# Two transformer blocks on one core: the order of ScalarE's and VectorE's work between the heads of the third block

## The chip, the cores and the metric

The kernel runs on one core of a Trainium2 chip. The metric is the device time of the whole kernel in microseconds, as the median of several runs; lower is better. TensorE, VectorE, ScalarE, GpSimd and SyncE each run their own program in order and meet at semaphores.

## The reference, cut to what matters

The input is one sequence of 256 tokens of width 1024, with a memory of 256 tokens of the same width. A first part (two layers with HGRN2 mixing and chunk-band attention, each followed by a SwiGLU) comes before the stretch that the change touches. The part that it touches is this (fp32 throughout):

```
proj = rms_norm(x) @ w_in            # q (8 heads of 64), k and v (2 heads), u, g
u, g = gelu(proj[u]), gelu(proj[g])
attn = sliding_window_attention(rms_norm(q), rms_norm(k), v, sinks)
sg   = u * spatial_gating(rms_norm(g))
x    = x + concat(rms_norm(attn), rms_norm(sg)) @ w_out
q    = rms_norm(rms_norm(x) @ w_cq)  # 4 heads of 256
k, v = rms_norm(mem_n @ w_ck), mem_n @ w_cv    # mem_n = rms_norm(mem)
x    = x + softmax(q k^T / 16) v @ w_co
x    = x + moe(rms_norm(x))          # 32 experts, 2 per token
```

## The kernel before

Every linear layer is computed from pieces of 128 output columns. A piece of weights comes from HBM into a ring of six slots (two pieces each). ScalarE rounds it to a high half (`hi_upto`, line 807), VectorE subtracts to get the low half (`lo_upto`, line 1268), and TensorE makes three products for each of eight chunks (48 matmuls for two pieces, lines 1999, 2023 and 2045). There are four buffers of split pieces, so the split of piece w can start when TensorE is done with piece w-4. Two result banks `lin` take turns; a pair of pieces must be drained by ScalarE or VectorE before the next pair but one can begin.

The activation operand `u` is also in two halves: ScalarE writes the high one and counts `u_hi`, VectorE the low one and counts `u_lo`.

The third block is called W, the cross attention X. TensorE's program goes through the heads of W two at a time: `scores_two`, a transpose of the probabilities (`turn_`, line 2309), `outputs_two` (line 2356). Between heads it does the 16 pieces `FILL` (keys `ck`, then values `cv`, of the memory), the spatial gates (lines 2522 and 2527) and sums of squares: FILL 0 and 1 after the first scores, 2 and 3 after turn 0, the gates after turn 1, 4 and 5 after turn 2, 6 and 7 after turn 3, 8 and 9 after turn 4, 10 and 11 after turn 5, 12 and 13 after turn 6, 14 and 15 after the last outputs. In the text "FILL n" is the nth of these pieces, and "pair n" is FILL 2n and 2n+1. The change leaves TensorE's program as it is.

For a head of W, VectorE scales and masks the scores and takes maxima (`scores`, lines 1584 to 1600), ScalarE does the exponentials (`exps`, line 973), VectorE divides (`probs`, lines 1609 and 1612), TensorE turns, ScalarE copies the turned block (`copy`, line 984) and later takes an output pair (`drain`, line 1154's group). Between heads both engines call `between_w(i)`, which ends with splits of the next FILL pieces and, on ScalarE, with `memory(i)`, which drains finished pairs: a square and a copy for the keys (lines 1070 and 1071), a copy for the values (line 1074). How far they may go at i is given by

```
def filled(i):
    return 2 * (i + 2) if i < 1 else min(2 * (i + 1), 14) if i < HW else 16
```

Before W, `in2_act` drains the seven pairs of the input projection; the last is a gelu (line 1116). Then ScalarE writes the memory operand (line 1122) and VectorE its low half (line 1742). After W come the output projection `out2` (`add_gated`, line 1351), the norm `cross`, the queries `cq` and X, whose keys need six steps `key_norm(0)` to `key_norm(5)` on VectorE: four reciprocals (line 1701) and two products (line 1705). TensorE's first X scores (line 2299) wait for both products.

Of the kernel before, what the change touches and what calls it, by code (L numbers as in the profile page):

```python
# [29 lines left out]
DC = D // P  # L30
# [174 lines left out]
def two_blocks(nc, x, c, mod_w, mod_b, norm_mix, norm_ffn, ffn_w_in, ffn_w_out, a_w_in, a_w_out, a_lb,  # L205
# [15 lines left out]
    with ExitStack() as ctx:  # L221
# [575 lines left out]
        def _(act):  # L797
# [164 lines left out]
            def attention_act(kind, hi_out, between=lambda i: None):  # L962
# [30 lines left out]
                if kind == "X":  # L993
                    for i in range(n + 2):
                        if i < n:
                            exps(i)
                        if 1 <= i <= n:
                            copy(i - 1)
                        if i >= 2:
                            drain(i - 2)  # L1000
                        between(i)
                    return
                for j in range(n // 2 + 1):
# [59 lines left out]
            def memory(i):  # L1063

                hi_upto(min(FILL[0]["w"] + filled(min(i - 1, HW)) + 3, LAST["cv"] + 2))
                while 2 * drained[0] + 2 <= min(filled(min(i - 1, HW)), 14):
# [23 lines left out]
            def in2_act():  # L1090
                for n, pair in enumerate(pairs("in2")):
                    if n == 6:
                        act.wait_ge(w_dup, 1)
                        act.activation(kdup, acc[:, 0:2, :], ACT.Copy).then_inc(w_dc, 1)
                    result(pair)
# [21 lines left out]

            in2_act()
            wait_out(act, jobs["in2"][-1])
            act.wait_ge(x_tc, 2)  # L1120
            for c_ in range(DC):
                act.activation(u[:, 0, c_, :], memT[:, c_, :], ACT.Copy, scale=vec("norm_mem_2", c_)).then_inc(u_hi, 1)

            def between_w(i):

                if i == 0:
                    for b in range(TB):
# [132 lines left out]
        def _(dve):  # L1260
# [79 lines left out]
            def add_gated(job, gate):  # L1340

                for n, pair in enumerate(pairs(job)):
# [13 lines left out]
                    ins.then_inc(lin_out["dve"], 1)  # L1356
                    if job == "a_out" and n < 2:
# [216 lines left out]
            def attention_dve(kind, lo_out, between=lambda i: None):  # L1574
# [46 lines left out]
                if kind == "X":  # L1621
                    scores(0)
                    for i in range(n + 2):
                        if i == 1:
                            probs(i)
                        if i + 1 < n:
                            scores(i + 1)
                        if i < n and i != 1:
                            probs(i)
                        if i >= 2:  # L1630
                            drain(i - 2)
                        between(i)
# [105 lines left out]
            lo_upto(LAST["in2"] + LOOKAHEAD)  # L1738
# [6 lines left out]
            wait_out(dve, jobs["in2"][-1])  # L1745
# [3 lines left out]
            def between_w(i):  # L1749

                if i == 0:
                    dve.wait_ge(w_std, 3)
# [33 lines left out]
            attention_dve("W", None, between_w)  # L1786
# [8 lines left out]
            for n, p in enumerate(jobs["cq"][:6]):  # L1795
                lo_upto(p["w"] + LOOKAHEAD)
                key_norm(n)
# [7 lines left out]
                lambda i: lo_upto(jobs["co"][(1, 3)[i]]["w"]) if i < 2 else None)  # L1805
# [998 lines left out]
```

## Time and profile before

| | |
|---|---|
| median of 3 runs | 1487.49 us (1486.2 to 1488.25) |
| the profiled execution | 1483.92 us, span 1481.9 us |
| TensorE matmul busy | 1437.8 us, 97% of the span |
| VectorE busy | 755.2 us, 51% |
| ScalarE busy | 565.2 us, 38% |
| mean granted TensorE clock | 0.986 |
| moved from and to HBM | 404.14 MB, mean 273 GB/s |

TensorE is busy nearly all the time. The third block begins near 820 us of the span, the output projection near 900, the cross attention near 950 and the experts near 1030. In the timeline a row gives the start, the busy time, the engine, the line, and in brackets the idle time just before it and what ended it. The granted clock is a share of 2.4 GHz: 1.00 is 2.4 and 0.50 is 1.2.

### The profile page before, as it was taken

The numbers are of one execution on the slowest core, as the hardware profiler recorded it, in microseconds if no ns is written. First come the engines' busy times: TensorE is split into PE (matmuls) and PEld (weight loads), VectorE is DVE, ScalarE is ACT, GpSimd is POOL, SyncE is SP. The second block draws the span as 40 slices with busy tenths as digits, with TensorE's granted clock in tenths as the row PEclk, the third lists the DMA queues.
The fourth block names the chain that finished last, engine by engine and source line by source line (L and its number), as shares of the span: only waits on it lengthen the run. The fifth ranks groups of instructions, "written<-read, shape, count | busy, mean of one in ns | idle before, by whom it ended". The sixth has DMA issues, their size and how long they took to land. (4 is left out here: it accounts for less than half of the span.)

```text
span 1481.9 us, 26323 instructions
## 1 busy us (share of the span) xinstructions
PE 1437.8 (97%) x11240; PEld 1211.5 (82%) x11240; DVE 755.2 (51%) x1194; ACT 565.2 (38%) x885; POOL 28.6 (2%) x47
## 2 busy tenths in 40 slices
PE   7999999999999999999999899999999999999997
PEld 4998899999999879999999789888666566566664
DVE  3968767876776656555555655644122122122121
ACT  2522235343454555444444664451212212212211
POOL 0100000000001010000000000010000000000000
PEclk9999999999999999999999999999999999999999
DMA  9996455979769514665645336426999999999996
GB/s 370 309 322 211 155 174 196 328 279 319 280 225 327 177 52 164 207 222 204 210 132 168 118 114 236 163 62 253 413 424 427 425 427 425 428 427 425 426 425 263
DMA packets 155378, 404.14 MB, mean 273 GB/s; under 512 B 5107, under 2 KB 123152, under 8 KB 133906
## 3 DMA queue, kind: packets, MB, share of 16 engines
q1 hardware_dynamic: 152960, 396.90, 71.1%
q0 software_dynamic: 1648, 5.18, 1.2%
q8 instruction: 76, 1.25, 0.4%
q10 hardware_dynamic: 674, 0.64, 0.1%
q14 instruction: 20, 0.16, 0.0%
HBM read 401.63 MB, written 1.07 MB: 272 GB/s over the span
## 5 line engine op out<-in xcount | busy, mean ns | idle before, releaser
L1999 PE MATMUL ps<-u,wsplit 128*128 128x256 f32 x3744 | 461.7, 284 | 5.3 <-DVE wsplit L1268 5.3
L1999 PEld LDWEIGHTS ps<-u,wsplit 128*128 128x128 f32 x3744 | 452.8, 192 | 11.9 <-DVE wsplit L1268 6.4
L1268 DVE TENSOR_TENSOR wsplit<-arena,wsplit 128x1024 fp32r<-128x1024 f32 x258 | 312.5, 1226 | 198.7 <-ACT wsplit L807 198.5
L807 ACT ACTIVATE wsplit<-arena 128x1024 fp32r<-128x1024 f32 x258 | 270.1, 1056 | 294.9 <-PE ps L1999 150.8
L2666 PE MATMUL ps<-arena 128*64 128x256 f32 x1408 | 155.9, 379 | 1.1 <-DVE arena L1897 0.8
L2666 PEld LDWEIGHTS ps<-arena 128*64 128x64 f32 x1408 | 101.6, 137 | 60.8 <-issue 12.6
L1902 DVE TENSOR_TENSOR arena<-arena,ps 128x256 f32<-128x256 f32 x32 | 13.5, 422 | 235.9 <-ACT arena L1216 223.8
L2261 PE MATMUL ps<-hid,wsplit 128*128 128x256 f32 x1056 | 130.7, 283 | 0.3 <-DVE hid L1524 0.3
L2261 PEld LDWEIGHTS ps<-hid,wsplit 128*128 128x128 f32 x1056 | 128.3, 192 | 0.5 <-DVE hid L1524 0.5
L1221 ACT ACTIVATE arena<-ps 64x512 f32<-64x512 f32 x62 | 36.6, 591 | 141.4 <-PE ps L2688 140.7
L2045 PE MATMUL ps<-wsplit,u 128*128 128x256 f32 x672 | 83.2, 284 | 1.8 <-ACT arena L1074 1.6
L2045 PEld LDWEIGHTS ps<-wsplit,u 128*128 128x128 f32 x672 | 81.3, 192 | 2.9 <-DVE wsplit L1268 2.2
L2688 PE MATMUL ps<-arena 128*64 128x512 f32 x336 | 76.7, 598 | 0.5 <-ACT arena L1218 0.5
L2666 PE MATMUL ps<-late,arena 128*64 128x256 f32 x640 | 71.0, 379 | 1.0 <-DMA late<-in_w 1.0
L1336 DVE SCALAR_TENSOR_TENSOR arena<-arena,cact 128x2048 f32<-128x2048 f32 (+1 forms) x33 | 70.1, 2125 | 0.2
L2666 PEld LDWEIGHTS ps<-late,arena 128*64 128x64 f32 x640 | 45.8, 137 | 28.8 <-issue 5.6
L1216 ACT ACTIVATE arena<-ps 128x256 f32<-128x256 f32 x31 | 11.9, 384 | 148.2 <-PE ps L2666 148.2
L2023 PE MATMUL ps<-u,wsplit 128*128 128x256 f32 x480 | 61.0, 287 | 5.0 <-DVE u L1742 2.1
L2023 PEld LDWEIGHTS ps<-u,wsplit 128*128 128x128 f32 x480 | 59.0, 191 | 7.5 <-DVE wsplit L1268 3.9
L2651 PEld LDWEIGHTS ps<-arena 128*128 128x128 f32 x512 | 59.5, 192 | 5.8 <-issue 5.8
L2651 PE MATMUL ps<-arena 128*128 128x128 f32 x512 | 63.8, 278 | 0.0
L1912 DVE SCALAR_TENSOR_TENSOR y_split<-arena,y_split 128x1024 fp32r<-128x1024 f32 x15 | 19.3, 1285 | 80.7 <-ACT y_split L1228 80.7
(369 smaller groups left out, 1376.3 us busy)
## 6 DMA issues: line engine op xcount, KB each, us to landing
arena<-in_w SPq DMA_DIRECT2D x64, 2048.0 KB, 22.4
late<-in_w SPq DMA_DIRECT2D x30, 2048.0 KB, 23.5
arena<-in_mod_w SPq DMA_DIRECT2D x48, 1024.0 KB, 7.0
arena<-in_ffn_w_in SPq DMA_DIRECT2D x44, 1024.0 KB, 5.9
arena<-in_ffn_w_out SPq DMA_DIRECT2D x22, 1024.0 KB, 5.0
arena<-in_a_w_in SPq DMA_DIRECT2D x16, 1024.0 KB, 8.6
arena<-in_kv_mod_w SPq DMA_DIRECT2D x8, 1024.0 KB, 4.9
arena<-in_kv_w SPq DMA_DIRECT2D x8, 1024.0 KB, 7.2
```

The source lines that it names most:

```text
L807: act.activation(piece_buf(p, 0), piece_src(p), ACT.Copy).then_inc(hi_done, 1)
L1221: act.activation(y_sb[64 * k:64 * k + 64, 512 * j:512 * (j + 1)], ps[64 * j:64 * j + 64, 6, :], ACT.Copy).then_inc(m_yc, 1)
L1268: dve.tensor_tensor(piece_buf(p, 1), piece_src(p), piece_buf(p, 0).bitcast(F32), ALU.subtract).then_inc(lo_done, 1)
L1336: ins = dve.scalar_tensor_tensor(out=total, in0=rows, scalar=cact[:, k, 7:8], in1=total, op0=ALU.mult, op1=ALU.add)
L1912: dve.scalar_tensor_tensor(out=y_split[:, 1, :], in0=y_sb, scalar=slot_gate, in1=y_split[:, 0, :].bitcast(F32), op0=ALU.mult, op1=ALU.subt ...
L1999: mm = pe.matmul(o, w_[:, k, :], u[:, x_, k, :], start=first, stop=last)
L2023: mm = pe.matmul(lin[p["out"] % 2][:, p["half"], :], piece_buf(p, lo)[:, k, :], u[:, x_, k, :], start=(at == 0 and n == 0 and p["half"] == 0),
L2045: mm = pe.matmul(lin[p["out"] % 2][:, b, :].rearrange("p (c n) -> p c n", c=2), u[:, x_, k, P * b:P * (b + 1)], wsplit[:, first_buf:first_ ...
L2261: mm = pe.matmul(acc[:, c_, :], piece_buf(p, lo)[:, k, P * jj:P * (jj + 1)], hid[:, fi % 2, x_, k, :], start=(i == 1 and c_ % 2 == 0 and k ...
L2651: mm = pe.matmul(ps[:, 6 + half, P * c_:P * (c_ + 1)], hn_tok[:, b, P * (4 * half + c_):P * (4 * half + c_ + 1)], sel[:, b, :], start=(b = ...
L2666: mm = pe.matmul(ps[64 * j:64 * j + 64, 0, 256 * m:256 * (m + 1)], xe[:, c_, own], w13[w_][:, m, c_, 256 * j:256 * (j + 1)], start=(c_ == ...
L2688: mm = pe.matmul(ps[64 * j:64 * j + 64, 6, :], tt[:, P * m + 64 * jk:P * m + 64 * jk + 64], w2b[w_][:, 2 * jk + m, 512 * j:512 * (j + 1)], ...
```

## The change

The instructions stay the same in kind and number; their order on ScalarE and VectorE changes.

- ScalarE's order in W is written out by itself: exp i, copy i-2, drain, then what was between heads i-1 and i. VectorE's order likewise: both scores, probs of the even head, the work between of the head before, probs of the odd head, the work between of the even head.
- The low split of FILL 2 (and no further) comes between the first two scores and their probs; that of FILL 3 stands at the head of `between_w(0)` on both engines, ahead of the squares and the root.
- ScalarE writes the memory operand ahead of the last split and the last gelu of the input projection.
- `memory(0)` drains pair 0 and pair 1, where it drained pair 0 alone.
- Three of the six `key_norm` steps go into the additions of `out2`, the other three behind the first three splits of the queries.
- In X, VectorE does probs 2 before scores 3, and splits one piece of `co` after each of heads 0, 1 and 2, where it split two at head 0 (up to piece 1) and head 1 (up to piece 3).

```
--- before.py
+++ after.py
@@ -1000,6 +1000,17 @@
                             drain(i - 2)
                         between(i)
                     return
+                if kind == "W":
+                    for i in range(n + 3):
+                        if i < n:
+                            exps(i)
+                        if 2 <= i < n + 2:
+                            copy(i - 2)
+                        if i >= 4 and i % 2 == 0:
+                            drain(i - 3)
+                        if i >= 1:
+                            between(i - 1)
+                    return
                 for j in range(n // 2 + 1):
                     for i in (2 * j, 2 * j + 1):
                         if i < n:
@@ -1063,7 +1074,7 @@
             def memory(i):
 
                 hi_upto(min(FILL[0]["w"] + filled(min(i - 1, HW)) + 3, LAST["cv"] + 2))
-                while 2 * drained[0] + 2 <= min(filled(min(i - 1, HW)), 14):
+                while 2 * drained[0] + 2 <= min(filled(min(max(i - 1, 0), HW)), 14):
                     n, pair = drained[0], FILL[2 * drained[0]:2 * drained[0] + 2]
                     act.wait_ge(piece_done, pair[1]["w"] + 1)
                     if n < 4:
@@ -1092,6 +1103,8 @@
                     if n == 6:
                         act.wait_ge(w_dup, 1)
                         act.activation(kdup, acc[:, 0:2, :], ACT.Copy).then_inc(w_dc, 1)
+                        hi_upto(pair[0]["w"] + LOOKAHEAD)
+                        memory_hi(pair[1]["w"])
                     result(pair)
                     if n == 0:
                         act.wait_ge(u_lo, 48)
@@ -1115,15 +1128,21 @@
                         m = n - 5
                         act.activation(gW[:, :, 256 * m:256 * (m + 1)], bank(pair), ACT.Gelu_apprx_tanh).then_inc(lin_out["act"], 1)
 
+            def memory_hi(after):
+
+                act.wait_ge(piece_done, after + 1)
+                act.wait_ge(x_tc, 2)
+                for c_ in range(DC):
+                    act.activation(u[:, 0, c_, :], memT[:, c_, :], ACT.Copy, scale=vec("norm_mem_2", c_))\
+                        .then_inc(u_hi, 1)
+
             in2_act()
-            wait_out(act, jobs["in2"][-1])
-            act.wait_ge(x_tc, 2)
-            for c_ in range(DC):
-                act.activation(u[:, 0, c_, :], memT[:, c_, :], ACT.Copy, scale=vec("norm_mem_2", c_)).then_inc(u_hi, 1)
 
             def between_w(i):
 
                 if i == 0:
+                    hi_upto(FILL[3]["w"])
+                    wait_out(act, jobs["in2"][-1])
                     for b in range(TB):
                         act.activation(gn[:, b, :], gW[:, b, :], ACT.Square, accum_out=gst[:, b:b + 1])\
                             .then_inc(w_sq, 1)
@@ -1354,6 +1373,8 @@
                         if n == 3 and m == 0:
                             ins.then_inc(h_first, 1)
                     ins.then_inc(lin_out["dve"], 1)
+                    if job == "out2" and n < 3:
+                        key_norm(n)
                     if job == "a_out" and n < 2:
                         weighted_rows(jobs["rows_out"][n])
 
@@ -1571,7 +1592,7 @@
             dve.wait_ge(mod_done, 4)
             ffn_dve(0, "ffn0", lambda c_: gain[:, 1, c_:c_ + 1], lambda c_: mod[:, 24 + c_:25 + c_],
                     lambda c_: mod[:, 40 + c_:41 + c_], lambda i: new_gains() if i == FFI - 1 else None)
-            def attention_dve(kind, lo_out, between=lambda i: None):
+            def attention_dve(kind, lo_out, between=lambda i: None, split_first=lambda: None):
                 first, n = FIRST[kind], COUNT[kind]
                 r0, r1, every = runs(kind)
 
@@ -1621,14 +1642,28 @@
                 if kind == "X":
                     scores(0)
                     for i in range(n + 2):
-                        if i == 1:
+                        if i in (1, 2):
                             probs(i)
                         if i + 1 < n:
                             scores(i + 1)
-                        if i < n and i != 1:
+                        if i < n and i not in (1, 2):
                             probs(i)
                         if i >= 2:
                             drain(i - 2)
+                        between(i)
+                    return
+                if kind == "W":
+                    for j in range(n // 2):
+                        scores(2 * j)
+                        scores(2 * j + 1)
+                        if j == 0:
+                            split_first()
+                        probs(2 * j)
+                        if j > 0:
+                            between(2 * j - 1)
+                        probs(2 * j + 1)
+                        between(2 * j)
+                    for i in (n - 1, n, n + 1):
                         between(i)
                     return
                 for j in range(n // 2 + 1):
@@ -1735,20 +1770,21 @@
             dve.wait_ge(w_rs, 1)
             dve.scalar_tensor_tensor(out=kW, in0=k_raw, scalar=vec("k_norm_2"), in1=k_std,
                                      op0=ALU.mult, op1=ALU.mult).then_inc(w_n, 1)
-            lo_upto(LAST["in2"] + LOOKAHEAD)
+            lo_upto(FILL[1]["w"])
             dve.wait_ge(x_tc, 2)
             for c_ in range(DC):
                 dve.wait_ge(u_hi, 8 * OPERANDS["mem"] + c_ + 1)
                 dve.scalar_tensor_tensor(out=u[:, 1, c_, :], in0=memT[:, c_, :], scalar=vec("norm_mem_2", c_),
                                          in1=u[:, 0, c_, :].bitcast(F32), op0=ALU.mult, op1=ALU.subtract)\
                    .then_inc(u_lo, 1)
-            wait_out(dve, jobs["in2"][-1])
             dve.wait_ge(w_ms, 8)
             dve.wait_ge(w_n, 2)
 
             def between_w(i):
 
                 if i == 0:
+                    lo_upto(FILL[3]["w"])
+                    wait_out(dve, jobs["in2"][-1])
                     dve.wait_ge(w_std, 3)
                     dve.reciprocal(gst[:, 4:6], gst[:, 2:4]).then_inc(w_rs, 1)
                     dve.wait_ge(w_rs, 2)
@@ -1783,7 +1819,7 @@
                         dve.scalar_tensor_tensor(out=sq[:, c_, :], in0=mix[:, c_, :], scalar=vec("out_norm_attn_2", c_),
                                                  in1=half_std[:, 0, :], op0=ALU.mult, op1=ALU.mult).then_inc(scaled, 1)
 
-            attention_dve("W", None, between_w)
+            attention_dve("W", None, between_w, lambda: lo_upto(FILL[2]["w"]))
             for n, c_ in enumerate(MIXED):
                 dve.wait_ge(u_hi, 8 * OPERANDS["mixed"] + n + 1)
                 dve.tensor_tensor(u[:, 1, c_, :], sq[:, c_, :], u[:, 0, c_, :].bitcast(F32), ALU.subtract)\
@@ -1794,7 +1830,8 @@
             operand("cross", h, lambda c_: vec("norm_cross_2", c_), None)
             for n, p in enumerate(jobs["cq"][:6]):
                 lo_upto(p["w"] + LOOKAHEAD)
-                key_norm(n)
+                if n < 3:
+                    key_norm(3 + n)
 
             dve.wait_ge(x_std, 2)
             dve.reciprocal(q_rstd[:, 0:4], stat[:, 16:20]).then_inc(x_rs, 1)
@@ -1802,7 +1839,7 @@
             attention_dve("X", lambda i, o: dve.tensor_tensor(
                 u[:, 1, 2 * i:2 * i + 2, :], o.rearrange("p (c t) -> p c t", c=2),
                 u[:, 0, 2 * i:2 * i + 2, :].bitcast(F32), ALU.subtract),
-                lambda i: lo_upto(jobs["co"][(1, 3)[i]]["w"]) if i < 2 else None)
+                lambda i: lo_upto(jobs["co"][1 + i]["w"]) if i < 3 else None)
             add_gated("co", None)
 
             norm_rstd("moe")
```

## Rows read from the trace of the kernel before

**Rows 1.** Timeline of TensorE near the end of the experts.
```profile
1433.53 3.67 PE L2666 MATMUL ps<-late,arena 128*64 128x256 f32 x32 [0.98 <-DMA late<-in_w]
```

**Rows 2.** Timeline of SyncE's DMA issues, first load after expert 0 began.
```profile
1033.57 0.36 SPq L638 DMA_DIRECT2D arena<-in_w  x1
```

**Rows 3.** Timeline of TensorE in the W stage.
```profile
823.11 5.99 PE L2023 MATMUL ps<-u,wsplit 128*128 128x256 f32 x48 [2.10 <-DVE u L1742]
829.19 0.55 PE L2309 MATMUL ps<-ident,arena 128*128 128x128 f32 x3
...
836.01 3.14 PE L1999 MATMUL ps<-u,wsplit 128*128 128x256 f32 x24 [2.36 <-DVE wsplit L1268]
...
845.02 0.60 PE L2309 MATMUL ps<-ident,arena 128*128 128x128 f32 x3 [1.39 <-DVE arena L1612]
...
848.61 6.10 PE L1999 MATMUL ps<-u,wsplit 128*128 128x256 f32 x48
...
860.61 0.51 PE L2309 MATMUL ps<-ident,arena 128*128 128x128 f32 x3
...
862.71 6.01 PE L2045 MATMUL ps<-wsplit,u 128*128 128x256 f32 x48
...
879.21 5.99 PE L2045 MATMUL ps<-wsplit,u 128*128 128x256 f32 x48 [1.55 <-ACT arena L1074]
...
888.59 0.87 PE L2356 MATMUL ps<-arena 128*64 128x256 f32 x8 [1.34 <-ACT arena L984]
```

**Rows 4.** Windows of 2 us: busy by engine, then granted clock, DMA share, GB/s.
```profile
846.00:848.00 2.00, 2.00 (x12) 1.00 (x12) 1.30 (x3) 0.00 (x0) 0.00 (x0) 0.50 0.18 55
...
952.00:954.00 2.00, 2.00 (x5) 1.64 (x6) 0.00 (x0) 1.35 (x2) 0.00 (x0) 0.50 1.05 451
...
976.00:978.00 2.00, 2.00 (x7) 1.58 (x6) 0.00 (x0) 0.00 (x0) 0.00 (x0) 0.50 1.00 426
```

**Rows 5.** Timeline of ScalarE at the start of the W stage.
```profile
820.25 1.06 ACT L807 ACTIVATE wsplit<-arena 128x1024 fp32r<-128x1024 f32 x1 [3.98 <-PE ps L2045]
...
821.82 3.31 ACT L1122 ACTIVATE u<-arena,vec 128x256 fp32r<-128x256 f32 x8
...
828.51 0.41 ACT L973 ACTIVATE arena<-arena,small 128x129 f32<-128x129 f32 x1 [0.38 <-DVE small L1600]
...
829.40 0.61 ACT L1128 ACTIVATE arena<-arena 128x512 f32<-128x512 f32 x1
...
833.66 2.94 ACT L807 ACTIVATE wsplit<-arena 128x1024 fp32r<-128x1024 f32 x3
```

**Rows 6.** Timeline of VectorE in the W stage.
```profile
825.65 0.17 DVE L1584 COPY arena<-arena 128x2 f32<-128x2 f32 x1
...
828.39 0.15 DVE L1609 RECIPROCAL small<-small 128x2 f32<-128x2 f32 x1
...
846.02 1.28 DVE L1765 TENSOR_TENSOR arena<-ps,arena 128x512 f32<-128x512 f32 x2
```

**Rows 7.** Timeline of TensorE in the cross attention.
```profile
951.84 6.76 PE L2299 MATMUL ps<-arena,late 128*128 128x256 f32 x16 [1.89 <-DVE arena L1705]
...
965.46 1.89 PE L2299 MATMUL ps<-arena,late 128*128 128x256 f32 x8
...
974.22 0.66 PE L2309 MATMUL ps<-ident,arena 128*128 128x128 f32 x4 [2.13 <-DVE arena L1612]
974.72 3.26 PE L2323 MATMUL ps<-arena 128*128 128x256 f32 x8
```

**Rows 8.** Timeline of VectorE from the output projection to the cross attention.
```profile
910.36 2.36 DVE L1268 TENSOR_TENSOR wsplit<-arena,wsplit 128x1024 fp32r<-128x1024 f32 x2 [1.74 <-ACT wsplit L807]
...
937.24 1.74 DVE L1701 RECIPROCAL arena<-arena 128x256 f32<-128x256 f32 x1
...
948.18 1.27 DVE L1705 SCALAR_TENSOR_TENSOR arena<-arena,vec 128x1024 f32<-128x1024 f32 x1
...
972.50 0.75 DVE L1600 TENSOR_REDUCE small<-ps 128x1 f32<-128x256 f32 x2
```

More of the change, by code:

```diff
@@ L1002, in attention_act @@
                     return
+                if kind == "W":
+                    for i in range(n + 3):
+                        if i < n:
+                            exps(i)
+                        if 2 <= i < n + 2:
+                            copy(i - 2)
+                        if i >= 4 and i % 2 == 0:
+                            drain(i - 3)
+                        if i >= 1:
+                            between(i - 1)
+                    return
                 for j in range(n // 2 + 1):
@@ L1094, in in2_act @@
                         act.activation(kdup, acc[:, 0:2, :], ACT.Copy).then_inc(w_dc, 1)
+                        hi_upto(pair[0]["w"] + LOOKAHEAD)
+                        memory_hi(pair[1]["w"])
                     result(pair)
@@ L1116, in in2_act, with memory_hi @@
                         act.activation(gW[:, :, 256 * m:256 * (m + 1)], bank(pair), ACT.Gelu_apprx_tanh).then_inc(lin_out["act"], 1)
+            def memory_hi(after):
+                act.wait_ge(piece_done, after + 1)
+                act.wait_ge(x_tc, 2)
+                for c_ in range(DC):
+                    act.activation(u[:, 0, c_, :], memT[:, c_, :], ACT.Copy, scale=vec("norm_mem_2", c_))\
+                        .then_inc(u_hi, 1)
             in2_act()
[L1119 to L1122, printed above, removed]
             def between_w(i):
                 if i == 0:
+                    hi_upto(FILL[3]["w"])
+                    wait_out(act, jobs["in2"][-1])
                     for b in range(TB):
@@ L1356, in add_gated @@
                     ins.then_inc(lin_out["dve"], 1)
+                    if job == "out2" and n < 3:
+                        key_norm(n)
                     if job == "a_out" and n < 2:
@@ L1627, in attention_dve @@
                             scores(i + 1)
-                        if i < n and i != 1:
+                        if i < n and i not in (1, 2):
                             probs(i)
@@ L1631, in attention_dve @@
                             drain(i - 2)
+                        between(i)
+                    return
+                if kind == "W":
+                    for j in range(n // 2):
+                        scores(2 * j)
+                        scores(2 * j + 1)
+                        if j == 0:
+                            split_first()
+                        probs(2 * j)
+                        if j > 0:
+                            between(2 * j - 1)
+                        probs(2 * j + 1)
+                        between(2 * j)
+                    for i in (n - 1, n, n + 1):
                         between(i)
@@ L1737, in _ @@
                                      op0=ALU.mult, op1=ALU.mult).then_inc(w_n, 1)
-            lo_upto(LAST["in2"] + LOOKAHEAD)
+            lo_upto(FILL[1]["w"])
             dve.wait_ge(x_tc, 2)
@@ L1751, in between_w @@
                 if i == 0:
+                    lo_upto(FILL[3]["w"])
+                    wait_out(dve, jobs["in2"][-1])
                     dve.wait_ge(w_std, 3)
@@ L1796, in _ @@
                 lo_upto(p["w"] + LOOKAHEAD)
-                key_norm(n)
+                if n < 3:
+                    key_norm(3 + n)
             dve.wait_ge(x_std, 2)
```

11 lines of the change are left out of this document (5 added, 6 removed).

## The prediction

> **What bounds the kernel now.** I began with the chain that ended last and the experts stage, because they decide whether a gain in the third block can reach the end. TensorE is the bound. In the experts each new load is issued when TensorE has finished part of an expert, the first of these at 1033.57, and TensorE waits for a weight load only near the end, 0.98 us at 1433.5 [rows 1, 2]. TensorE and the load queue thus both start from the moment at which TensorE reaches expert 0, so what is gained before 1030 us is carried to the end; the reader is to see that the load at 1033.57 hangs on TensorE and not on a time of its own.
>
> Next the timeline of TensorE in the third block. Its idle stretches from the sliding-window heads to the last FILL piece are 2.10 us before the first memory piece, 2.36 before the fourth, 1.39 before turn 2, 1.55 before pieces 12 and 13, 1.34 before the outputs of heads 6 and 7 [rows 3]. In the cross attention they are 1.89 us before scores 0 and 2.13 before turn 2 [rows 7]. Then the table of windows, for the granted clock: after three of these seven idle stretches (1.39, 1.89, 2.13) it reads 0.50, which is 1.2 GHz, for some microseconds [rows 4]. After the 2.10, 2.36, 1.55 and 1.34 it did not fall. The same turn, scores and outputs take 848.61 - 845.02 = 3.59 us at the lower level and 862.71 - 860.61 = 2.10 at the higher, so that fall cost 1.49 [rows 3]. The 16 score matmuls of the cross attention took 6.76 against 2 x 1.89 = 3.78, 2.98 more, and the 8 output matmuls after the last stall 3.26 against 1.89, 1.37 more [rows 7].
>
> **Part 1, memory operand ahead of the last gelu.** The instructions are the same. ScalarE is free at 820.25 and spends 1.57 us on the split of FILL 2 and the gelu before the eight conversions begin at 821.82 [rows 5]. After the change the first conversion starts at 820.25; VectorE follows about 0.45 behind and TensorE another 0.55, near 821.3 instead of 823.11: a gain of 1.8. Behind it on ScalarE the total work is equal (8 conversions 3.31, split, gelu), so the exponentials of heads 0 and 1 are not later on that account.
>
> **Part 2, what VectorE does next.** It loses the low split of FILL 2 in front and has it back between scores 1 and probs 0 (1.14 us pitch). Conversions end about 824.1, two scores take 828.39 - 825.65 = 2.74 (to 826.8), the split ends 827.95, and probs 0, 0.75 long, end at 828.7. ScalarE has its table at 826.45 and the exponentials of two heads, 0.9 each (829.40 - 828.51), by 828.3, so they are in time [rows 5, 6]. TensorE ends FILL 0 and 1 at 821.3 + 6.0 = 827.3 and stands until 828.8. So of the 1.8 only 0.4 is left: turn 0 at 828.8 against 829.19 [rows 3]. That is the stall's new place.
>
> **Part 3, split of FILL 3 before the squares.** Now ScalarE's three splits start 4.26 us after the last exponential (829.40 to 833.66), held by two squares, the root and two table loads, and TensorE waits 2.36 [rows 5, 3]. After the change the split of FILL 3 comes at 828.3 (ScalarE) and is done on VectorE about 830.6, TensorE asks for it at 833.2. All 2.36 go, and FILL 3 ends near 836.1 instead of 839.0.
>
> **Part 4, second pair drained behind the first, and the order one head late.** ScalarE reaches FILL 4 and 5 at 828.3 + 1.0 + 4.26 = 833.6, the first drain at 835.55 and the second at 836.6. A drain is two activations of 512 columns, by the row at 829.40 at most 0.61 each, about 1.0 together [rows 5]. The second needs FILL 3 done, 836.1, so it waits for nothing. Turn 1 and the gates now take 4.6 us, from the end of FILL 3 at 839.0 to 843.6 (845.02 - 1.39) [rows 3]; after the change they end at 836.1 + 4.6 + 0.1 for the first drain, 840.8. Turn 2 needs probs 2, which VectorE has at 840.4, since scores 2 and 3 no longer stand behind the splits of FILL 6 and 7. What is late next is the copy of head 1: ScalarE does exp 2, copy 0, two splits, exp 3, copy 1 (0.95 + 0.45 + 1.9 + 0.9 + 0.45 = 4.65 us from 838.4), to 843.05. TensorE has its scores at 842.05, waits 1.1, does the outputs, waits 0.65 for the gate product (0.64 each, behind probs 3), and starts FILL 4 at 844.6 against 848.61 [rows 3, 6]. Gain so far, if the clock stays up: 4.0.
>
> From there TensorE is dense to FILL 11. The 1.55 us stall was for the drain of pair 5, which stood behind exp 7, copy 5 and a drain; after the change ScalarE splits FILL 14 and 15 right when FILL 11 is done and drains 0.4 us before TensorE asks: gain 1.55. At the outputs of heads 6 and 7 only copy 7 is left behind two splits and the drain, 0.95 of the 1.34 stays: gain 0.4. Sum of the W stage: 4.0 + 1.55 + 0.4 = 5.95 without any fall of the clock after the change. With one: the two waits of 1.75 together, with 64-column gate matmuls before them, look like the 1.39 us stall before which the clock fell, so I take one fall again, priced by the same row at 1.5. **W stage: 4.45.**
>
> **Part 5, key reciprocals.** Now VectorE alternates six splits of 1.1 to 1.2 with four reciprocals of 1.74 and two products of 1.27 from 936 on, all in front of scores 0, and is the last to be ready [rows 8, 7]. Three reciprocals move into the out2 additions: 3 x 1.74 = 5.2 us there, in gaps like the 1.74 us before the split at 910.36, in which VectorE waits for ScalarE [rows 8]; so at most 0.1 is late, for pieces that TensorE wants some 5 us later. Cost nothing; without that cover 1.74 each. The two products end near 943.6 on today's axis, scores 0 may start at 949.95. Gain 1.89 and, as no idle stands there, the 2.98 of low clock. **4.87.** Nothing excludes that another cause starts a fall there (the query sums before it are one column wide); bounds 1.89 and 4.87, the upper one taken, because the stall was part of every fall seen here.
>
> **Part 6, probs 2 before scores 3, one split less before it.** VectorE does scores 3 first (from 972.50, two reductions and a product of the maxima, 0.86) and probs 2 behind it [rows 8]. ScalarE's exponential of head 2 is ready by then; it has the same chain behind the last query pair before and after, and ends about 972.4 on today's axis. After: probs 2 about 0.95 earlier, the stall before turn 2 is 1.15 instead of 2.13. Scores 3 and the split of co 3 have over 3 us before turn 3 and the second half of the output chunk. Whether the clock stays up after 1.15 us: 1.55 and 2.36 did not bring it down, so I take yes, gain 1.37 and an estimated 0.28 for the chunk behind it. Bounds 0.98 and 2.6. **2.6.**
>
> **The sum.** 4.45 + 4.87 + 2.6 = 11.9 us. The profiled execution took 1483.92 (span 1481.9), which makes 1472.0; the median of the runs shown is 3.6 above that execution, and the same difference on it gives 1487.5 - 11.9 = **1475.6**.
>
> **The skill's rule on the clock.** The Trainium skill, TensorE: Matmul & The Clock Gate, Part 1: The HAM clock gate, says that half rate is the default and only activity releases it. Read strictly it speaks against this change, since new idle stretches appear at 827 and 842. This trace agrees only in part: three of seven stalls were followed by 1.2 GHz. By the rule the sum would be that of rival 2.
>
> **Rivals.** (1) No fall of the clock in the W stage: 1.5 more, 1474.1. For it: four of seven stalls were harmless. Against it: the gates. (2) Each stall that stays brings the clock down: 827 (1.5 us), 842, 882 (0.95), the unchanged one before out2, and turn 2 in the cross attention. That is three more falls in the W stage at 1.5 and the 1.65 of part 6: 11.9 - 6.2 = 5.7 us gained, 1481.8. (3) The gain doesn't reach the end: if the experts' loads had a pace not tied to TensorE, the 0.98 us wait at 1433 would grow by what was gained and the time stays at 1487.5. Against it: the load at 1033.57 is released by TensorE [rows 2]. (4) Slower: the new order on ScalarE. Its chain exp, copy, two splits, exp, copy is 4.65 us per pair of heads, and TensorE's scores, turns and outputs need it. If TensorE were to wait for the whole of it in all four pairs (the drain of pair 1 holding ScalarE until FILL 3 is done, and so on), that is 18.6 us against 13.4 gained: 1492.7. It decides against the change once 3.3 us per pair are exposed; I have 1.1 exposed in the first pair and none in the next two, because FILL pieces of 6 us lie between.
>
> **Chances.** Forecast as worked (within about 2 us) 0.5; rival 1 0.18; rival 2 or a part of it 0.2; rival 3 0.05; rival 4 0.03; 0.04 for a wait that I have not seen which takes back more than half, with a quarter of it on the slower side. The range 1472.5 to 1482 holds the first three. A change of 0.2% (3 us) is about what a measurement of this kernel can tell from none. Faster 0.91, same 0.05, slower 0.04.
>
> **What would show it.** TensorE's idle before the first memory piece 0.3 and before turn 0 1.5; none before FILL 3; about 1.1 and 0.65 before and after the first outputs; none before pieces 12 and 13; FILL 4 starting some 24 us after the first W scores instead of 28.5; scores 0 of the cross attention without a wait, at 1.00 clock, 3.8 us for 16 matmuls; turn 2 waiting about 1.15. The experts unchanged but earlier. It would be wrong if ScalarE's waits for TensorE grow (the drain of pair 1 before FILL 3 is done), if the clock falls in new places, or if the final load wait grows.

## The result and the profile after

The changed kernel takes 1468.17 us (median of 4 runs, 1467.60 to 1468.39), the kernel before 1486.85 beside it (4 runs, 1479.72 to 1488.25, three of them those shown before). The ratio is 0.9883, with a 95% interval of 0.9851 to 0.9915: 1.2% faster. The forecast was 1475.6, with a range of 1472.5 to 1482.0, so the time lies 4.3 us under the range. Timed again (e9 below) the ratio was 0.9896, interval 0.9875 to 0.9918.

Timeline of TensorE in the W stage, the changed kernel; these rows answer to [rows 3]:

```profile
818.15 0.93 PE L2377 MATMUL ps<-arena 64*128 64x128 f32 x8
819.50 5.99 PE L2060 MATMUL ps<-u,wsplit 128*128 128x256 f32 x48 [0.42 <-DVE u L1777]
826.72 0.55 PE L2346 MATMUL ps<-ident,arena 128*128 128x128 f32 x3 [1.23 <-DVE arena L1633]
...
828.05 6.01 PE L2036 MATMUL ps<-u,wsplit 128*128 128x256 f32 x48
833.90 0.49 PE L2346 MATMUL ps<-ident,arena 128*128 128x128 f32 x3
...
837.58 1.97 PE L2564 MATMUL ps<-arena 128*64 128x128 f32 x16
839.48 0.90 PE L2346 MATMUL ps<-ident,arena 128*128 128x128 f32 x3
...
842.33 5.99 PE L2036 MATMUL ps<-u,wsplit 128*128 128x256 f32 x48
...
871.19 6.02 PE L2082 MATMUL ps<-wsplit,u 128*128 128x256 f32 x48
...
880.23 0.87 PE L2393 MATMUL ps<-arena 128*64 128x256 f32 x8 [0.96 <-ACT arena L984]
...
891.55 5.98 PE L2060 MATMUL ps<-u,wsplit 128*128 128x256 f32 x48 [1.06 <-DVE u L1825]
```

The waits before FILL 3 and FILL 12 are gone, the one before FILL 0 is 0.42, and a new one of 1.23 stands before turn 0. The same timeline in the cross attention, answering to [rows 7]:

```profile
941.43 3.70 PE L2336 MATMUL ps<-arena,late 128*128 128x256 f32 x16
...
959.87 0.66 PE L2346 MATMUL ps<-ident,arena 128*128 128x128 f32 x4 [1.24 <-DVE arena L1633]
960.36 1.89 PE L2360 MATMUL ps<-arena 128*128 128x256 f32 x8
```

Scores 0 start without a wait and at full clock, and the outputs behind turn 2 take 1.89 where they took 3.26. The table of windows, answering to [rows 4], has the only low clock from the W stage to the experts here:

```profile
836.00:838.00 2.00, 2.00 (x18) 1.07 (x16) 1.93 (x9) 1.78 (x6) 0.00 (x0) 0.90 0.83 291
838.00:840.00 2.00, 2.00 (x19) 1.65 (x15) 1.65 (x3) 2.00 (x5) 0.00 (x0) 0.50 0.65 228
840.00:842.00 2.00, 2.00 (x16) 1.21 (x16) 1.96 (x5) 0.73 (x3) 0.00 (x0) 0.75 0.00 0
```

The profiled executions took 1483.92 us before (span 1481.9) and 1467.60 after (span 1465.5). The 16.4 us between the spans, taken from starts of the same instructions in both timelines:

| stretch of TensorE's timeline | before | after | gained | forecast |
|---|---|---|---|---|
| start to the first W scores | 820.08 | 818.15 | 1.93 | 0 |
| to FILL 4 | 28.53 | 24.18 | 4.35 | 2.5 |
| to FILL 12 | 30.60 | 28.86 | 1.74 | 1.55 |
| to the output projection | 20.70 | 20.36 | 0.34 | 0.4 |
| to scores 0 of the cross attention | 51.93 | 49.88 | 2.05 | 1.89 |
| to turn 2 there | 22.38 | 18.44 | 3.94 | 3.96 |
| to expert 0 | 55.45 | 53.54 | 1.91 | 1.65 |
| to the end | 452.2 | 452.1 | 0.1 | 0 |

The first row has nothing to do with the change, which touches no instruction of that stretch: in the 17 profiled executions below and here the first W scores start anywhere from 815.2 (e10) to 820.1 us (before), in changed and unchanged kernels alike. In the other rows 14.4 us were gained against 11.9 forecast.

### The profile page after: what moved, and what is told of

The parts are those of the page before. It is cut to its first block and busy times, and to the rows that moved or that the text cites. A ratio compares the mean times of both kernels' runs of the same rounds, so it can differ in the third digit from the quotient of the medians.

```text
span 1465.5 us, 26324 instructions
## 1 busy us (share of the span) xinstructions
PE 1431.3 (98%) x11240; PEld 1205.9 (82%) x11240; DVE 755.0 (52%) x1194; ACT 564.8 (39%) x885; POOL 28.6 (2%) x47
## 5 line engine op out<-in xcount | busy, mean ns | idle before, releaser
L2082 PEld LDWEIGHTS ps<-wsplit,u 128*128 128x128 f32 x672 | 81.3, 192 | 1.3 <-issue 0.7
L1235 ACT ACTIVATE arena<-ps 128x256 f32<-128x256 f32 x31 | 11.9, 385 | 148.3 <-PE ps L2703 148.3
```

Of the source, the lines that this page charges most:

```text
L2082: mm = pe.matmul(lin[p["out"] % 2][:, b, :].rearrange("p (c n) -> p c n", c=2), u[:, x_, k, P * b:P * (b + 1)], wsplit[:, first_buf:first_ ...
```

## Experiments

In the comparisons below "W stage" is the time in the profile from TensorE's first W scores to the first matmul of the output projection: 79.8 us before, 73.4 after. "Clock" is the mean granted TensorE clock of an execution, which every timed run has. The runs fall into four groups, and each group has its own runs of the kernel before, timed beside it; ratios are taken within a group. A gain "by ratio" is the ratio's distance from 1 times the median of before.

Several experiments put filler matmuls into a wait of TensorE. `warm(pair, n)` is a helper that the kernel has already: it issues n matmuls of 128x256 whose result nobody reads.

**First group: the two halves, and one stall filled.** e1 is the changed kernel without the key reciprocals and the order in X:

```
-                    if job == "out2" and n < 3:
-                        key_norm(n)
...
-                        if i in (1, 2):
+                        if i == 1:
...
-                if n < 3:
-                    key_norm(3 + n)
+                key_norm(n)
...
-                lambda i: lo_upto(jobs["co"][1 + i]["w"]) if i < 3 else None)
+                lambda i: lo_upto(jobs["co"][(1, 3)[i]]["w"]) if i < 2 else None)
```

e2 is the kernel before with these same edits the other way round, e3 the kernel before with the two on `key_norm` alone. e4 adds a line to the kernel before:

```
+            warm(jobs["cq"][6:], 8)
             pe.wait_ge(x_n, 2)
             pe.wait_ge(x_std, 1)
             attention_pe("X", ...
```

e1: 

> The changes of the W stage alone (memory operand first, splits, second drain, order of ScalarE and VectorE); key reciprocals and the order in the cross attention as in the kernel before. Theory (the gains add up, each stall on its own): by the two traces the W stage gave 6.4 us between the first W scores and the output projection, so 6 to 7 us less than before, with the 1.89 and 2.13 us stalls of the cross attention and 1.2 GHz behind both still there. Rival (the gain hangs together: the two falls of the clock in the cross attention depend on when they are met): 3 to 10 us, with a clock row of 1.00 behind one of them.

e2: 

> Key reciprocals moved and the new order in the cross attention, on the kernel before; W stage untouched. Theory: 7.65 us less than before (2.05 the stall before scores 0, 3.06 its low clock, 0.9 the stall before turn 2, 1.65 its low clock). Rival: if the times of several runs of the kernel before differ because its falls of the clock differ, the gain in the median is larger, 9 to 12 us, and its runs lie closer together than those of before.

e3: 

> Only the key reciprocals moved. Theory: 5 us less than before, scores 0 of the cross attention without a wait and at 1.00 clock; the 2.13 us stall before turn 2 and the fall behind it stay. Rival: without the first fall the second doesn't come either, 6.7 us less.

e4: 

> The kernel before with eight matmuls of zeros (128x256) put on TensorE where it waits 1.89 us for the key products; nothing else is changed, their result is never read. Theory (the idle stretch brings the clock down, and the low clock costs more than the wait): the wait is filled, the 16 score matmuls run at 1.00 and take 3.8 us instead of 6.8, 3 us less than before. Rival (the narrow query sums ahead bring it down, or the fall isn't worth its row): 0 to 0.5 us.

| | median (runs) | ratio to before, interval | clock, median | W stage |
|---|---|---|---|---|
| before | 1485.53 (27) | | 0.985 | |
| e1, W only | 1472.19 (6) | 0.9924, 0.9898 to 0.9951 | 0.9895 | 74.9 |
| e2, X only | 1475.08 (10) | 0.9946, 0.9926 to 0.9966 | 0.989 | 82.8 |
| e3, keys only | 1481.30 (12) | 0.9981, 0.9964 to 0.9998 | 0.9875 | 81.3 |
| e4, eight fillers | 1483.62 (12) | 0.9997, 0.9979 to 1.0015 | 0.988 | 82.7 |

By ratio e1 gives 11.3 us (interval 7.3 to 15.2), above both its theory, 6 to 7, and its rival's 10, and e2 8.0 (5.0 to 11.0), where its theory said 7.65 and its rival 9 to 12. e3 gives 2.8 (0.3 to 5.3), less than its theory, 5, and its rival, 6.7. Yet in e3's timeline scores 0 of the cross attention wait for nothing and take 3.70, as its theory had it, and no fall follows the 2.15 us before turn 2, as its rival had it. The interest is in the last column: e2, e3 and e4 have the W stage of before unaltered, and it takes 1.5 to 3 us more than in the execution from which the prediction was made. The timeline of e2 shows where, at FILL 3:

```profile
834.03 4.64 PE L2002 MATMUL ps<-u,wsplit 128*128 128x256 f32 x24 [2.36 <-DVE wsplit L1268]
```

The same wait of 2.36 us as in [rows 3], the same 24 matmuls, 4.64 us for 3.14: behind it the clock fell, which it had not done there. In e1 it is the other way round, in the cross attention. The clock stays up there behind both waits, as its rival had it for one of them:

```profile
945.16 3.72 PE L2333 MATMUL ps<-arena,late 128*128 128x256 f32 x16 [1.89 <-DVE arena L1738]
964.50 0.66 PE L2343 MATMUL ps<-ident,arena 128*128 128x128 f32 x4 [2.13 <-DVE arena L1631]
```

The 1.89 us wait stands and the scores run at full clock (6.76 in [rows 7]). e4 gives 0.4 us by ratio (at most 3.1), where its theory had said 3 and its rival 0 to 0.5. It overran the wait: the eight fillers make 16 records of 3.7 us in all, so the scores began 1.65 late, which is more than half of the 3.1 that they won (3.62 for 6.76). The clock of e4 rose, its time hardly gained.

**Second group: fillers of the right size, a shift, the operand late.** e5 is e4 with 4 for the 8. e6 has fillers in four waits of the kernel before: ahead of FILL 3, behind the gates, ahead of turn 2 in X and ahead of scores 0 there:

```
+            def busy(n):
+                for _ in range(n):
+                    pe.matmul(rbc, ident[:], cact[:].rearrange("p k n -> p (k n)")[:, 0:T], start=True, stop=True)
...
+                        if n == 3:
+                            busy(5)
                         linear(FILL[n])
...
                         mm.then_inc(w_s, 1)
+                    busy(3)
...
+                elif i == 1:
+                    warm(jobs["co"], 4)
...
+            warm(jobs["cq"][6:], 4)
             pe.wait_ge(x_n, 2)
```

e7 shifts the changed kernel (ScalarE's lines, then VectorE's):

```
-                        if i >= 1:
+                        if i == 1 or i > 2:
+                            if i == 3:
+                                between(1)
                             between(i - 1)
...
+                        probs(2 * j)
                         if j == 0:
                             split_first()
-                        probs(2 * j)
-                        if j > 0:
+                        if j > 1:
                             between(2 * j - 1)
```

e8 puts the memory operand of the changed kernel back behind the last gelu:

```
-                        hi_upto(pair[0]["w"] + LOOKAHEAD)
-                        memory_hi(pair[1]["w"])
...
             in2_act()
+            memory_hi(LAST["in2"])
```

e5: 

> The kernel before with four idle-filling matmuls (128x256, of an identity and a nearly empty tile, result never read) where TensorE waits for the key products, in place of the eight tried first, which took 3.7 us in a stretch of 1.9. Theory (the fall of the clock is a cost of its own beside the wait): the wait is filled to the end and not overrun, scores 0 run at 1.00, 2.5 to 3.5 us less in the median. Rival (the fall only moves to the next stall): 0 to 1 us.

e6: 

> The kernel before with such matmuls in four of its waits: five before FILL 3, three before turn 2 of the W stage, four before scores 0 and four before turn 2 of the cross attention. No wait is shortened. Theory (a part of what the change gave is falls of the clock behind these waits, and their number differs from run to run): 7 to 9 us less in the median, mean granted clock 0.990 or more, and runs within 3 us instead of 11. Rival (the spread and the lower median of before come from elsewhere, such as the first loads): 3 to 5 us less, spread as before.

e7: 

> The changed kernel with two shifts in the W stage. VectorE: low split of FILL 2 behind probs 0, and the gate product directly behind probs 3. ScalarE: exponentials and copy of head 1's successor (exp 3, copy 1) ahead of the high splits of FILL 6 and 7. Theory (turn 0 waits for the split in front of probs 0, the first outputs for copy 1 and the gate product): 0.7 us less before turn 0, 1 to 1.7 us less before FILL 4, so 1.5 to 2.5 us faster than the changed kernel. Rival (low clock covers these waits): under 0.7 us in all.

e8: 

> The changed kernel with the memory operand written by ScalarE behind the last split and gelu again. Theory (the prediction's part 2: the gain of the early operand mostly returns as the stall before turn 0): first memory piece 1.6 us later, turn 0 0 to 0.5 us later, whole kernel 0 to 0.5 us slower than the changed one. Rival (the early operand is worth its whole stall): 1.5 to 2 us slower.

| | median (runs) | ratio to before, interval | clock, median | W stage |
|---|---|---|---|---|
| before | 1482.28 (23) | | 0.988 | |
| e5, four fillers | 1480.27 (12) | 0.9988, 0.9969 to 1.0006 | 0.9895 | 82.7 |
| e6, four waits filled | 1477.96 (12) | 0.9960, 0.9942 to 0.9978 | 0.992 | 78.3 |
| e7, two shifts | 1469.22 (6) | 0.9910, 0.9877 to 0.9942 | 0.991 | 74.9 |
| e8, operand late | 1469.67 (6) | 0.9918, 0.9888 to 0.9948 | 0.991 | 74.5 |

e6 is the clean test. It shortens no wait: FILL 3 starts 15.93 us after the first W scores in e6 and before, turn 2 24.93 and 24.94. The kernel before gets 0.40% faster by it, 5.9 us (3.3 to 8.6), with a clock of 0.992. The theory had said 7 to 9 us and runs within 3 us of one another, the rival 3 to 5 and a spread as before; it is 5.9, and the runs span 6.7 us where those of before span 12.8. e5 leans the same way, 1.8 us where 2.5 to 3.5 were expected, but its interval includes 1. e7 shows no gain on the changed kernel, where 1.5 to 2.5 us were expected: turn 0 waits 0.74 instead of 1.23, then TensorE waits 0.56 before the gates for ScalarE's drain, and the clock was low from 836.5 to 843.5. e8 contradicts my expectation in the timeline and bears out its rival:

```profile
816.76 0.93 PE L2376 MATMUL ps<-arena 64*128 64x128 f32 x8
819.59 5.98 PE L2059 MATMUL ps<-u,wsplit 128*128 128x256 f32 x48 [1.91 <-DVE u L1776]
826.81 0.55 PE L2345 MATMUL ps<-ident,arena 128*128 128x128 f32 x3 [1.24 <-DVE arena L1632]
```

Turn 0 comes 10.05 us after the first scores, against 8.57 in the changed kernel and 9.11 before. VectorE's scores and split behind the conversions are as late as the conversions, so the early operand is worth its 1.48 us there. The split of FILL 2 ahead of probs 0 costs 0.94 against the order of before, and 0.49 against its place behind probs 0 in e7. The times can't confirm it: the intervals of e8, e9 and the changed kernel's first runs overlap.

**Third group: the changed kernel again, one part undone at a time.** e9 is the changed kernel itself. The edits of e10 (the first), e11 (the next two) and e12 (the last), each alone:

```
-                while 2 * drained[0] + 2 <= min(filled(min(max(i - 1, 0), HW)), 14):
+                while 2 * drained[0] + 2 <= min(filled(min(i - 1, HW)), 14):
...
                 if i == 0:
-                    hi_upto(FILL[3]["w"])
...
                 if i == 0:
-                    lo_upto(FILL[3]["w"])
...
+            warm(jobs["co"][4:], 4)
             pe.wait_ge(route, CHOSEN)
```

e9: 

> The changed kernel once more, unaltered, beside the others of this call. Theory (its gain over my sum is low clock that the kernel before has in more places than its one profiled execution showed): median 1468 to 1470, runs within 4 us of one another, clock 0.990; span times clock 1452, as in its first runs. Rival (its first four runs were lucky): median 1471 or more and a spread like that of before.

e10: 

> The changed kernel with pair 0 alone drained in the first work between heads, as before the change. Theory (the order one head late makes the second drain late, so the change needs both together): the second gate product waits for the drain of pair 1, which comes behind exp 2, copy 0 and two splits; 3 to 5 us slower than the changed kernel. Rival (the waits behind it, for copy 1 and the gate product, absorb it): under 1 us.

e11: 

> The changed kernel with the split of FILL 3 behind the squares and the root again. Theory: TensorE waits 2.4 to 3 us before FILL 3, and this wait brings the clock down in part of the runs: 3 to 4.5 us slower in the median, clock lower by 0.001, spread wider. Rival (only the wait counts): 2.4 us, clock unchanged.

e12: 

> The changed kernel with four idle-filling matmuls (result never read) on TensorE while it waits 1.77 us for the routing, just ahead of the experts. In five of nine profiles the clock fell behind this wait and the transposes and gathers there took 2.7 us more. Theory: 1 to 2.7 us less than the changed kernel in the median. Rival (in the changed kernel the fall doesn't come here, as its own profile shows none): 0.

| | median (runs) | ratio to before, interval | clock, median | W stage |
|---|---|---|---|---|
| before | 1482.42 (11) | | 0.987 | |
| e9, changed kernel | 1468.90 (6) | 0.9896, 0.9875 to 0.9918 | 0.9905 | 73.4 |
| e10, one drain | 1473.93 (6) | 0.9940, 0.9920 to 0.9960 | 0.989 | 79.1 |
| e11, FILL 3 late | 1466.01 (6) | 0.9885, 0.9866 to 0.9904 | 0.994 | 74.1 |
| e12, router filled | 1468.09 (6) | 0.9902, 0.9883 to 0.9922 | 0.9915 | 73.4 |

e9 falls between theory and rival: the median held, but its runs span 6.9 us. e10 shows the second drain to be needed: without it the kernel is 5.0 us slower than e9 beside it, as expected, and one wait of TensorE before the second gate product stands out:

```profile
837.51 2.07 PE L2559 MATMUL ps<-arena 2*128 2x512 f32 x2 [3.90 <-ACT arena L1082]
```

e11 was expected 3 to 4.5 us slower and is not slower. TensorE waits 1.60 before FILL 3, but no fall follows, and the gates behind it run at full clock, so the W stage grows by 0.7 only. All six runs had a clock of 0.994. Where the trace of e11 does have low clock, it costs nothing: 32 matmuls of the router take 5.45 us in place of 3.82, and the wait for VectorE's routing behind them, 1.77 in the changed kernel, is gone. e12 gives nothing that its interval can tell.

**Fourth group: three questions left.** e13 is the kernel before with the `busy(5)` of e6 alone (e6's other fillers stand with 0 or are left out). e14 is e11 with e12's fillers and the low split of FILL 2 behind probs 0. e15 removes both `if kind == "W"` branches of the change and keeps `split_first` behind the first two scores:

```
e14
                         scores(2 * j + 1)
+                        probs(2 * j)
                         if j == 0:
                             split_first()
-                        probs(2 * j)
e15
-                if kind == "W":
-                    for i in range(n + 3):
...
-                if kind == "W":
-                    for j in range(n // 2):
...
                         scores(2 * j + 1)
+                        if j == 0:
+                            split_first()
                         probs(2 * j)
```

e13: 

> The kernel before with five idle-filling matmuls where TensorE waits 2.36 us for FILL 3, and nowhere else. In four later profiles of kernels whose W stage is that of before, the clock fell behind this wait, in the one that the prediction used it did not. Theory (this fall is what that profile lacked): W stage, from its first scores to the output projection, 80 us or less in the profile against 81.3 to 82.8; 1.5 to 2.5 us less in the median, waits as before. Rival (the fall only comes a little later in the W stage): 0 to 0.7 us.

e14: 

> The fastest variant so far (changed kernel, split of FILL 3 late again) with the low split of FILL 2 behind probs 0 and the router's wait filled. Theory: turn 0 0.7 us earlier but FILL 3 waits that much longer, so 0 from that; the router's wait was followed by no fall in that variant, so 0 from that too: 1465.5 to 1466.5. Rival (either shift moves a fall of the clock): 1468 or more.

e15: 

> The changed kernel with the order of before between the heads of the W stage on both engines; the early memory operand, the splits of FILL 2 and 3 and the second drain stay. Theory (the order one head late is what makes probs 2 ready for turn 2 and removes the wait before FILL 12): those two waits return, 1.4 and 1.5 us, and copy 1 is no longer waited for (0.4 less): 2 to 4 us slower than the changed kernel. Rival (the order only exchanges waits): within 1 us of it.

| | median (runs) | ratio to before, interval | clock, median | W stage |
|---|---|---|---|---|
| before | 1483.57 (16) | | 0.9865 | |
| e13, FILL 3's wait filled | 1478.66 (11) | 0.9969, 0.9952 to 0.9986 | 0.988 | 80.4 |
| e14, late and filled | 1469.37 (5) | 0.9907, 0.9887 to 0.9927 | 0.991 | 76.6 |
| e15, old order | 1472.84 (6) | 0.9929, 0.9909 to 0.9948 | 0.9905 | 79.4 |

e13 has the 24 matmuls of FILL 3 at full clock and gains 0.31%, 4.6 us (2.1 to 7.1), where 1.5 to 2.5 were expected; the W stage is 80.4, just above the line that I drew:

```profile
834.88 3.15 PE L1999 MATMUL ps<-u,wsplit 128*128 128x256 f32 x24 [0.19 <-DVE wsplit L1268]
```

Part of what it saves returns in the same profile: gate 2 takes 1.62 for 1.09. e14 doesn't keep e11's clock: FILL 3 waited 2.09 us and took 4.50 behind it, and the rival's time holds. A sixth run of e14 took 2856 us and is left out of its row; why is open. e15 makes the order one head late worth some 4.9 us by the ratios (0.9929 against 0.9896 of e9, whose intervals overlap), where 2 to 4 were expected, and 6.0 us of W stage in the profiles: turn 2 waits 3.43, longer than in any other profile here, for probs 2 behind the splits of FILL 6 and 7. The wait before FILL 12, 1.54 at 878.77, is back.

```profile
844.00 0.90 PE L2323 MATMUL ps<-ident,arena 128*128 128x128 f32 x3 [3.43 <-DVE arena L1622]
```

**What the clock is worth in a run.** The kernel before was timed 77 times with its clock in the four groups:

| clock | 0.984 | 0.985 | 0.986 | 0.987 | 0.989 | 0.991 |
|---|---|---|---|---|---|---|
| runs | 15 | 14 | 11 | 11 | 8 | 12 |
| mean, us | 1486.9 | 1485.3 | 1483.7 | 1483.4 | 1481.0 | 1477.8 |

(0.983, 0.988 and 0.990 had 6 runs.) From 0.984 to 0.991 the time falls by 9.1 us; 0.007 of 1480 is 10.4. So most of the run-to-run spread of this kernel goes with its clock. Span times clock takes it out, as an estimate: 1461.7 for the kernel before (mean of the 77), 1452.1 and 1453.5 for the changed one (medians of its two sets). By that, 8 to 10 us of the gain are waits. The mean clock rose from 0.9868 to 0.9905 and 0.9913, which is another 5.5 to 6.7 us of 1480.

## Why the prediction was right in kind and too small

The forecast was 7.4 us too high: 2.5 in the terms of the sum, 1.9 in the stretch ahead of the change, 3.0 in the last line, which turned the profiled execution into a median.

**What held.** Most of TensorE's moves are those that were worked out: turn 0 waits 1.23 (1.5 said), FILL 3 waits for nothing, FILL 12 waits for nothing, the outputs of heads 6 and 7 wait 0.96 (0.95), turn 2 in X 1.24 (1.15), scores 0 take 3.70 at full clock (3.8). The experts are the same length, 452.1 against 452.2, so rival 3 is out: everything gained ahead of 1030 reached the end. Rival 4 is out in that form, though e10 and e15 show its mechanism: with either half of the new order missing, a single wait of 3.4 to 3.9 us appears. Rival 1, no fall in the W stage, is not what the profile shows, though its W stage is even shorter than that rival had it.

**Part 4 was mis-sized, 2.5 where 4.35 was measured to FILL 4.** I took one fall of the clock again at its full 1.5 us and beside it 1.75 us of waits, 1.1 for copy 1 and 0.65 for the gate product. The profile has the fall and neither wait. Gate 2 takes 1.97 for 1.09, turn 2 0.90 for 0.49, the scores 1.24 for 0.93: 1.6 us of slow matmuls, after which copy 1 and the gate product were ready. e8 has the same stretch without a fall, and there both waits stand, 0.53 and 0.68:

```profile
840.50 0.87 PE L2392 MATMUL ps<-arena 128*64 128x256 f32 x8 [0.53 <-ACT arena L984]
842.05 5.99 PE L2035 MATMUL ps<-u,wsplit 128*128 128x256 f32 x48 [0.68 <-DVE arena L1800]
```

From turn 1 to FILL 4 it is 8.05 us in e8 and 8.43 in the changed kernel, so this fall cost 0.4 and not 1.5. Slow matmuls and a wait for another engine in the same stretch are not a sum; the first fills the second. It is also luck how far the fall reaches: in the changed kernel's two profiles and e12's it ended before the outputs, in e1 and e7 it covered them too (1.55 for 0.87) and FILL 4 came 1.2 us later. With that, the W stage gave 6.43 instead of 4.45 in the profile.

**A wait was not part of every fall.** Part 4 looked for the fall behind the two waits at 842, and part 5 took its upper bound because "the stall was part of every fall seen here". The changed kernel's fall began at 837.5, when TensorE had waited for 0.1 us in all since turn 0 at 826.72. The kernel before has such a fall too, which the prediction left out, in the router's matmuls ahead of the experts (timeline and table of windows):

```profile
1016.53 5.21 PE L2622 MATMUL ps<-arena,sq 128*128 128x128 f32 x32
...
1016.50:1017.00 0.50, 0.50 (x4) 0.50 (x4) 0.17 (x1) 0.00 (x0) 0.00 (x0) 0.50 1.15 492
```

It began near 1016, behind matmuls of 36 columns and with no wait since 994.3. It too cost little: the 32 matmuls took 1.39 us more than in the changed kernel (5.21 against 3.82), and the wait behind them was 0.41 instead of 1.77. For scores 0 the stall was the right thing to remove all the same: without it they ran at full clock in each of the eleven profiles that have no stall there.

**The anchor was 3.0 us too high.** The last line of the sum put the difference between the shown median, 1487.49, and the profiled execution, 3.6, unchanged on the result. After the change profile and median differ by 0.6 us. The 77 later runs show what the 3.6 was: their median is 1483.5, their median clock 0.986, as in the profiled execution, and only 15 of them took 1486.2 us or more, as all three runs shown did. The profiled execution was the typical one and the three runs were long ones; runs at 0.984 take 1486.9 us by the table.

**The typical execution has its low clock in other places than the one profile.** The profile didn't show the fall behind FILL 3's wait, which e2, e3, e4 and e5 have (W stage 81.3 to 82.8), and the change removes that wait. Against these four the W stage gained 7.9 to 9.4 us and not 6.4. e6 and e13 show that the falls are a cost of their own, since they win 5.9 and 4.6 us with every wait in place.

**Rival 2 took the rule of the Trainium skill (TensorE: Matmul & The Clock Gate, Part 1: The HAM clock gate), that half rate is the default and activity releases it, to mean a fall behind every idle stretch.** That is stricter than what the page says, and the runs disagree with it: the waits that stayed in the changed kernel, 1.23, 0.96, 1.06 and 1.24, had no fall behind them. Nor is a wait without a fall safe: 2.36 had none in one execution and one in four others.

**What stays open.** Why one execution has the fall and another has not; no run here sets that. Why the stretch ahead of W differs by up to 4.9 us from one profiled execution to another, 1.93 between the two compared. Why all six runs of e11 had a clock of 0.994, and why e1 gained 11.3 us and e3 only 2.8 in the ratio.

**A version that beats both** was not established. e11 had the lowest median, 1466.0 against 1468.9 for e9 beside it, but the intervals of their ratios overlap, and e14 with one small shift and the router's fillers did not have that clock again.

## What to carry to other kernels

Read the granted clock of several executions before you price a stall: one profile shows one draw of where the clock falls, and three runs can all be long ones. Don't carry the difference between a profile and such a median over to the result. A wait on TensorE is worth its length plus, in part of the runs, 1.4 to 3.0 us of half clock behind it, but a fall that lies in front of another engine's wait costs little (0.4 us here). When a change puts the work of two engines one step late, test its halves alone: here each without the other cost about 5 us.

## What was not expected of the hardware

The same instructions behind the same wait ran at 1.2 GHz in one execution and at 2.4 in another: FILL 3 behind 2.36 us took 3.14 in one profile and 4.64 in the next, scores 0 behind 1.89 us took 6.76, 5.26 (e13) and 3.72 (e1). The clock also fell with TensorE at work and no wait before it, at 837.5 in the changed kernel and near 1016 in the kernel before. Filling the idle time with matmuls whose result nobody reads made the kernel before 0.40% faster (0.9960, 0.9942 to 0.9978).
